# Decoder block with retrieved experts: four last rows fetched in halves, the last query-weight chunk moved into an up weight's place

## The chip, the cores and the metric

The kernel runs on one core of a Trainium2 chip. The metric is the device time of one execution in microseconds (us). TensorE (PE) multiplies matrices, VectorE (DVE) and ScalarE (ACT) work on tiles, GpSimd (POOL) issues the indirect gathers, SyncE (SP) issues the plain transfers, and 16 DMA engines move the bytes between HBM and SBUF.

## What is computed

One layer of a decoder block on 256 tokens of width 1024, in float32. The parts that matter here come late in it:

```python
mixed = jax.nn.sigmoid(g_a) * (y_a @ w_up_fox[l]) + jax.nn.sigmoid(g_b) * (y_b @ w_up_moba[l])
x = x + gate1 * (mixed @ w_out[l])
h2 = rms_norm(x, norm2_g[l]) * (1.0 + scale2) + shift2
x = x + gate2 * peer_ffn(h2, ...)
# peer_ffn, for each token:
q = h2 @ w_q                                  # 8 heads x 2 halves x 128
sc = einsum(q, sub_keys); s1, i1 = top_k(sc[0], 16); s2, i2 = top_k(sc[1], 16)
eid = the 16 best of the pairs (i1, i2)       # one expert of 16384 each
g = softmax of their scores
y = sum over 8 heads x 16 experts of g * gelu(h2 . u_tab[eid]) * v_tab[eid]
```

Each token thus reads 128 experts, each a U vector and a V vector of 1024 floats.

## The kernel before

The 256 tokens are two tiles (t = 0, 1) of 128, one token per partition. The first stages (modulation, input projection, attention) use matrix weights that SP streams through `ring`, four places of 2 MB. The last four such chunks are the two up weights (places 2 and 3 of `ring`) and the two output weights (places 0 and 1).

**Rows.** The experts are handled as `ROWS` = 256 rows: row n is, for every token of tile n // 128, its expert number n % 128. A gather brings U and V of one row for 128 tokens, 1 MB (8 KB per partition), into one *place*. For each row DVE takes the dot product of U with h2 (`dots`, L1010), ACT makes gelu, the weight and a diagonal matrix of it (L1285, L1290, L1297), and PE adds diagonal times V into `ps_y` (`add_rows`, L1611). ACT takes rows two at a time, and one at a time in the last four pairs (`ALONE`).

**Places.** `BUFFERS` lists the places with the row from which each takes part. `plan_buffers` deals them round: a place goes to the back of the line when it has been used, and a new one enters at the front at its row. A gather into a place used before waits until PE has added the row that it held (`s_added`); a first use waits for what occupied the memory (`await_first_use`). POOL issues all gathers in the order of rows, from one loop (L581). Places R0a to R3b are halves of the four places of `ring`; Ka and Kb are the memory `kz` of the keys of attention.

**Query weights.** `w_peer_q` comes in four chunks of 2 MB, loaded by SP (`peer_run`, L494). Chunk 0 lies in `K_chunk`, which is `kz`; chunk 3 comes into `kz` too, once the queries (t=1, m=1) have read chunk 0. Queries m = 2c and 2c+1 read chunk c. `SLOT` says before which pair of rows PE computes which queries: (0, 6) stands at pair 25, (1, 0) and (1, 1) at pairs 7 and 10, (1, 7) at pair 40.

**First rows.** After the queries (0, 0) `choose_first` (DVE) ranks the scores of head 0, and the first 8 experts follow from them. ACT had copied the scores from PSUM to `sc` before. Between there and the first row PE finishes tile 1: the up products `("up", 1, c, g)`, the turning of the mixed rows by `turn_wide(1, h)` (four transposes each, L1370, copied to SBUF by ACT at L1239) and `out_part(1, n)`, the items `("o", 1, 0)` and `("o", 1, 1)` (L1562). Place R2 is free after ("up", 1, 1, 0), R3 and G after ("up", 1, 1, 1), R0 after ("o", 1, 0), R1 after ("o", 1, 1), W and X when h2 of tile 1 is done.

**End.** The last `SPLIT` rows are gathered in halves: first U of each, then, behind all U, V of each. PE waits for V of such a row by `s_late_v`.

Of the kernel before, what the change touches and what calls it, by code (L numbers as in the profile page):

```python
# [14 lines left out]
P = 128  # L15
# [52 lines left out]
EARLY = 8  # L68
ROWS = 2 * HEADS * TOPK

SPLIT = 2

ALONE = 4

# [12 lines left out]
NORM2_ROOT = 1  # L87


BUFFERS = [("R2a", 0), ("R2b", 0), ("R3a", 0), ("R3b", 0), ("G", 0), ("R0a", 0), ("R0b", 0), ("R1a", 0),  # L90
           ("R1b", 0), ("W", 11), ("X", 12), ("V", 52), ("S", 53), ("E", 76), ("Ka", 88), ("Kb", 89)]


def plan_buffers():
# [79 lines left out]
def block_kernel(nc, x, small, b_ada, b_fgate, norm2_g, ada_t, in_t, up_t, out_t, peer_t, keys_t, peer_uv, out):  # L174
# [21 lines left out]
    with ExitStack() as ctx:  # L196
# [3 lines left out]
        def sem(name):  # L200
            return ctx.enter_context(nc.semaphore(name))

        ring = sb("ring", [P, NW, KD, 512])
# [14 lines left out]
        sc = sb("sc", [P, LISTS * P])  # L218
# [108 lines left out]
        def blocks_of(place):  # L327
# [3 lines left out]
                     [blocks_of(extra[:]), blocks_of(yT[:, 0].rearrange("p g b n -> p (g b n)")),  # L331
                      blocks_of(fx[:].rearrange("p a n -> p (a n)")),
                      blocks_of(score[:, 2].rearrange("p j n -> p (j n)"))],
                     [K_chunk]]
        peer_from = [[sum(run.shape[1] for run in runs[:r]) for r in range(len(runs) + 1)] for runs in peer_runs]

        def peer_block(m, k):
# [55 lines left out]
        s_sq4 = sem("x1_squares_summed")  # L393
        s_h2 = sem("h2_half_ready")
        s_warm = sem("root_of_one_ready")
        s_g0 = sem("top_scores_shifted")
        s_g1 = sem("top_scores_exp")
        s_eid = sem("expert_ids_ready")
# [21 lines left out]
        def await_item(eng, key):  # L420

            if key in turned_no:
                eng.wait_ge(s_turned, turned_no[key] + 1)
            else:
                eng.wait_ge(s_item, plan[key] + 1)
# [5 lines left out]
        def await_read(eng, key):  # L431

            if key in turned_no:
                eng.wait_ge(s_turned_read, turned_no[key] + 1)
            else:
                eng.wait_ge(s_bank[plan[key] % NB], plan[key] // NB + 1)
# [23 lines left out]
        def await_first_use(eng, name):  # L460

            if name in "VS":
                await_item(eng, ("qp", 1, 3))
            elif name == "E":
                await_item(eng, ("qp", 1, 5))
            elif name[0] == "K":
                await_item(eng, ("qp", 1, 7))
            elif name == "G":
                await_read(eng, ("up", 1, 1, 1))
            elif name in "WX":  # L470
                eng.wait_ge(s_h2, 2 * TILES)
            else:
                await_item(eng, {"0": ("o", 1, 0), "1": ("o", 1, 1), "2": ("up", 1, 1, 0), "3": ("up", 1, 1, 1)}[name[1]])

        def gates_done(u):

# [5 lines left out]
        @block.sync  # L482
        def _(sp):
            def chunk(n):
                what, m = chunks[n]
                if n >= NW:
                    await_chunk_read(sp, n - NW)
                dst = ring[:, n % NW, :, :]
                src = {"ada": ada_t, "z": in_t, "up": up_t, "out": out_t}[what][m]
                sp.dma_start(dst, src).then_inc(s_chunk[n % NW], 16)  # L490

            def peer_run(m, r):
                first, last = peer_from[m][r:r + 2]
                sp.dma_start(peer_runs[m][r], peer_t[m, :, first:last, :]).then_inc(s_peer[m], 16)  # L494

            sp.dma_start(sm[:], small).then_inc(s_small, 16)
            sp.dma_start(x_sb[:], x[0].rearrange("(t p) d -> p t d", p=P)).then_inc(s_x, 16)
            for n in range(ADA_FIRST - 1):
                chunk(n)
            n, part = ADA_FIRST - 1, KD // 2  # L500
            sp.dma_start(ring[:, n, 0:part, :], ada_t[n, :, 0:part, :]).then_inc(s_ada_half, 16)
            sp.dma_start(ring[:, n, part:KD, :], ada_t[n, :, part:KD, :]).then_inc(s_chunk[n], 16)
            sp.wait_ge(s_zero, 2)
            for r, at in zip(MOD_ROW, (2, 3, 4, 5)):
                sp.dma_start(rows[0:1, r, :], b_ada[0:1, at * D:(at + 1) * D]).then_inc(s_bias, 16)
            for n in range(ADA_FIRST, len(chunks)):
                chunk(n)
            await_block(sp, NZ * KD - 1)
            sp.dma_start(g2_row, norm2_g[0].partition_broadcast(P)).then_inc(s_g2, 16)
            sp.dma_start(skT[:], keys_t).then_inc(s_keys, 16)  # L510
            await_item(sp, ("S", 1, 1, HEAD_PAIRS - 1))
            sp.dma_start(x_sb[:], x[0].rearrange("(t p) d -> p t d", p=P)).then_inc(s_x, 16)
            peer_run(0, 0)
            await_item(sp, ("y", 1, 1, HEAD_PAIRS - 1))
            for r in range(2):
                peer_run(1, r)
            await_item(sp, ("up", 0, 1, 1))
            for r in range(1, 4):
                peer_run(2, r)
            sp.wait_ge(s_norm2_row, 1)  # L520
            peer_run(2, 0)
            await_item(sp, ("qp", 1, 1))
            peer_run(3, 0)
            for t in range(TILES):
                for h in range(2):
                    cut = slice(h * HALF, (h + 1) * HALF)
                    sp.wait_ge(s_yrow, 2 * t + h + 1)
                    sp.dma_start(out[0, t * P:(t + 1) * P, cut], x_sb[:, t, cut]).then_inc(s_stored, 16)
            sp.wait_ge(s_stored, 32 * TILES)
# [61 lines left out]
        def _(dve):  # L591
# [297 lines left out]

            def choose_first():  # L890

                await_read(dve, ("sc", 0, 0))
                for l in range(2):
                    ins = dve.max(v16[:, l, 0:EARLY], sc[:, l * P:(l + 1) * P])
                link(ins)
                for l in range(2):
                    ins = dve.max_index(i16[:, l, 0:EARLY], v16[:, l, 0:EARLY], sc[:, l * P:(l + 1) * P])
                link(ins)
                link(dve.tensor_copy(i16f[:, 0:2, 0:EARLY], i16[:, 0:2, 0:EARLY]))
                sums8 = flat[:, 0:EARLY * EARLY]  # L900
                link(dve.tensor_tensor(sums8.rearrange("p (a b) -> p a b", b=EARLY),
# [154 lines left out]
        def _(act):  # L1056
# [200 lines left out]
            def queries(t, m):  # L1257
                key = ("qp", t, m)
                await_item(act, key)
                read(act.activation(qp[:, m % 2, :, :],  # L1260
                                    bank(key)[:, 0:2 * P].rearrange("p (a n) -> p a n", n=P), ACT.Copy), key)
                if scored(t, m):
                    key = ("sc", t, m)
                    first, width = scored(t, m)[0], 2 * P * len(scored(t, m))
                    await_item(act, key)
                    if t:
                        act.wait_ge(s_eid, m + 2)
                    read(act.activation(sc[:, first * 2 * P:first * 2 * P + width],
                                        bank(key)[:, first % 2 * 2 * P:first % 2 * 2 * P + width], ACT.Copy), key)

# [78 lines left out]
        def _(pe):  # L1349
# [282 lines left out]
            up(1, 1, 0, first=1)  # L1632
            for c_ in range(2):
                up(1, c_, 1)
            for h in range(2):
                turn_wide(1, h)
            for n in range(2):
                out_part(1, n)
            for pair in range(NG * PAIRS):
                for stage in behind.get(pair, ()):  # L1640
                    stage()
# [53 lines left out]
```

## Time and profile before

| | |
|---|---|
| median of 3 runs | 904.52 us (904.2 to 905.95) |
| profiled execution: its time | 903.49 us |
| profiled execution: span from first to last instruction | 901.7 us |
| mean granted TensorE clock | 0.984 of full |
| PE busy | 772.4 us (86%) |
| DVE busy | 613.4 us (68%) |
| gathered by POOL's queue | 268.45 MB in 258 issues |
| mean transfer rate over the span | 373 GB/s |

All times in the text are counted from the start of the span. The time of an execution is 1.8 us above its span. A busy PE counts matmuls whose ends are modelled; the idle time of an engine that is not the bottleneck costs nothing.

### The profile page before, as it was taken

Reading aid. Unit: us, or ns where it says so; the run is one execution under the profiler, and the core shown is the slowest. Engines: PE = TensorE matmul, PEld = TensorE weight load, DVE = VectorE, ACT = ScalarE, POOL = GpSimd, SP = SyncE. Lnnn points to the kernel's source line nnn. Section 1 sums busy time; section 2 is a strip of 40 time slices with the busy share of each in tenths; the row PEclk is TensorE's granted clock in tenths of the full one; section 3 lists DMA queues with packets and bytes.
Section 4 is the critical chain, followed back from the end, with each engine's and each line's share of the span. In section 5 each row is a group of like instructions: output and inputs, shape, how many; then the busy total and the mean of one; then the engine's idle time right before and its main releaser. Section 6 shows DMA issues by size and latency. Waiting matters only on the chain.

```text
span 901.7 us, 8442 instructions
## 1 busy us (share of the span) xinstructions
PE 772.4 (86%) x2526; PEld 416.1 (46%) x2526; DVE 613.4 (68%) x1420; ACT 346.9 (38%) x1027; POOL 287.8 (32%) x279
## 2 busy tenths in 40 slices
PE   4999999999999999999997778687777777777777
PEld 2477777667556556565652333233322233222232
DVE  6788798954587967748669788768744444444445
ACT  3457688862144342422423242322422222222222
POOL 4000000000244444554636444353343334333320
PEclk9999999999999999999999989999999999999999
DMA  9977545679399999999999999999999999999995
GB/s 373 421 281 280 186 188 200 264 301 379 120 372 422 411 423 421 422 419 422 421 420 423 420 423 420 422 423 419 423 420 423 420 423 420 421 422 422 422 421 205
DMA packets 43812, 336.70 MB, mean 373 GB/s; under 512 B 4852, under 2 KB 4980, under 8 KB 7032
## 3 DMA queue, kind: packets, MB, share of 16 engines
q0 software_dynamic: 37152, 268.45, 71.9%
q1 hardware_dynamic: 6600, 67.72, 18.9%
q8 instruction: 20, 0.33, 0.1%
q14 instruction: 24, 0.20, 0.1%
q10 hardware_dynamic: 16, 0.00, 0.0%
HBM read 335.11 MB, written 1.05 MB: 373 GB/s over the span
## 4 chain that ended last, share of the span: by engine, by line
PE 47%; DMA 36%; DVE 10%; ACT 3%; issue 2%; POOL 1%; SPq 0%; DVEq 0%; ACTq 0%
DMA ring<-in_peer_uv,eid 26%; PE ps_y L1611 21%; DMA rows<-in_peer_uv,eid 6%; PE bank L1581 5%; DMA extra<-in_peer_uv,eid 4%; PE bank L1547 3%; DVE ring L1010 3%; PE bank L1422 2%; PE bank L1424 2%; PE bank L1423 2%; PE bank L1562 2%; PE ps_y L1422 1%; PE ps_y L1386 1%; PE ps_y L1424 1%; PE ps_y L1423 1%
## 5 line engine op out<-in xcount | busy, mean ns | idle before, releaser
L1611 PE MATMUL ps_y<-ring,diag 128*128 128x512 f32 x572 | 273.2, 617 | 58.2 <-ACT diag L1297 58.2
L581 POOL DMA_INDIRECT ring<-in_peer_uv,eid x142 | 150.1, 1057 | 414.8 <-DVE eid L916 227.0
L1010 DVE CUSTOM_DVE_ANT_0 ring<-ring,gates 128x1024 f32<-128x1024 f32 x143 | 173.2, 1224 | 101.8 <-DMA ring<-in_peer_uv,eid 101.0
L1611 PEld LDWEIGHTS ps_y<-ring,diag 128*128 128x128 f32 x572 | 108.0, 194 | 204.5 <-issue 116.8
L1285 ACT ACTIVATE mask<-mask 128x2 f32<-128x2 f32 (+1 forms) x132 | 26.7, 203 | 376.3 <-DVE mask L1010 376.1
L1297 ACT ACTIVATE diag<-ident,mask 128x128 f32<-128x128 f32 x256 | 87.3, 386 | 0.3
L1611 PE MATMUL ps_y<-rows,diag 128*128 128x512 f32 x136 | 63.8, 613 | 9.6 <-ACT diag L1297 9.6
L1290 ACT ACTIVATE mask<-g_sb,mask 128x1 f32<-128x1 f32 x256 | 61.9, 287 | 4.3
L1010 DVE CUSTOM_DVE_ANT_0 rows<-rows,gates 128x1024 f32<-128x1024 f32 x34 | 41.3, 1225 | 32.2 <-DMA rows<-in_peer_uv,eid 32.1
L645 DVE TENSOR_TENSOR w_lo<-ring,w_hi 128x512 fp32r<-128x512 f32 x76 | 50.6, 685 | 10.0 <-PE bank L1424 8.7
L1106 ACT ACTIVATE w_hi<-ring 128x512 fp32r<-128x512 f32 x76 | 45.6, 626 | 22.5 <-PE bank L1424 22.0
L581 POOL DMA_INDIRECT rows<-in_peer_uv,eid x34 | 37.8, 1111 | 31.2 <-PE ps_y L1611 26.7
L1611 PEld LDWEIGHTS ps_y<-rows,diag 128*128 128x128 f32 x136 | 25.6, 194 | 45.7 <-issue 27.3
L1611 PE MATMUL ps_y<-kz,diag 128*128 128x512 f32 x88 | 40.2, 599 | 7.5 <-ACT diag L1297 7.5
L1611 PE MATMUL ps_y<-gates,diag 128*128 128x512 f32 x72 | 34.8, 605 | 9.5 <-ACT diag L1297 9.5
L630 DVE SCALAR_TENSOR_TENSOR rows<-ring,silu,rows 128x512 f32<-128x512 f32 x56 | 41.9, 749 | 1.1
L1010 DVE CUSTOM_DVE_ANT_0 kz<-kz,gates 128x1024 f32<-128x1024 f32 x22 | 26.7, 1225 | 18.6 <-DMA kz<-in_peer_uv,eid 18.6
L1422 PE MATMUL bank<-w_hi,hT_hi 128*128 128x512 f32 x88 | 36.1, 410 | 0.0
L1424 PE MATMUL bank<-w_lo,hT_hi 128*128 128x512 f32 x88 | 34.3, 390 | 0.0
L1423 PE MATMUL bank<-w_hi,hT_lo 128*128 128x512 f32 x88 | 34.3, 390 | 0.0
L581 POOL DMA_INDIRECT kz<-in_peer_uv,eid x22 | 22.4, 1017 | 35.7 <-PE ps_y L1611 22.9
L1611 PE MATMUL ps_y<-spare,diag 128*128 128x512 f32 x52 | 25.2, 606 | 8.8 <-ACT diag L1297 7.6
(228 smaller groups left out, 1194.0 us busy)
## 6 DMA issues: line engine op xcount, KB each, us to landing
ring<-in_ada_t SPq DMA_DIRECT2D x11, 2048.0 KB, 9.6
ring<-in_in_t SPq DMA_DIRECT2D x10, 2048.0 KB, 10.1
ring<-in_up_t SPq DMA_DIRECT2D x2, 2048.0 KB, 8.7
ring<-in_out_t SPq DMA_DIRECT2D x2, 2048.0 KB, 13.7
kz<-in_peer_t SPq DMA_DIRECT2D x2, 2048.0 KB, 17.7
ring<-in_peer_uv,eid POOLq DMA_INDIRECT x142, 29.0
x_sb<-in_x SPq DMA_DIRECT2D x2, 1024.0 KB, 12.0
ring<-in_ada_t SPq DMA_DIRECT2D x2, 1024.0 KB, 21.3
```

Source lines behind the costliest of these rows:

```text
L581: pool.indirect_dma_start(uv_row(n), None, peer_uv, bass.IndirectOffsetOnAxis(ap=eid[:, n:n + 1], axis=0)).then_inc(s_uv[name], 16)
L630: ins = dve.scalar_tensor_tensor(out=acc, in0=w, scalar=silu[:, k:k + 1], in1=acc, op0=ALU.mult, op1=ALU.add)
L645: dve.tensor_tensor(w_lo[:, j % NLO, :], w, w_hi[:, j % NHI, :].bitcast(F32), ALU.subtract).then_inc(s_w_lo, 1)
L1010: dve.tensor_tensor_reduce(u_row(n), u_row(n), h2[:, n // P, :], 1.0, 0.0, ALU.mult, ALU.add, adot[:, at:at + 1]).then_inc(s_dot, 1)
L1106: act.activation(w_hi[:, j % NHI, :], ring[:, no % NW, k, :], ACT.Copy).then_inc(s_w_hi, 1)
L1290: act.activation(ew[:, c_:c_ + 1], g_sb[:, n:n + 1], ACT.Copy, scale=gel[:, c_:c_ + 1]).then_inc(s_ew, 1)
L1297: act.activation(diag[:, n % ND, :], ident[:], ACT.Copy, scale=ew[:, c_:c_ + 1]).then_inc(s_diag, 1)
L1422: pe.matmul(spot, hT_hi[:, k, at], hi, start=(k == 0), stop=False)
L1423: pe.matmul(spot, hT_lo[:, k, at], hi, start=False, stop=False)
L1424: ins = pe.matmul(spot, hT_hi[:, k, at], lo, start=False, stop=(k == KD - 1))
L1581: ins = pe.matmul(b[:, j * P:(j + 1) * P], peer_block(m // 2, k)[:, at:at + P], tT[:, t, k, :], start=(k == 0), stop=(k == KD - 1))
L1611: ins = pe.matmul(ps_y[:, cut], diag[:, n % ND, :], v_row(n)[:, cut], start=first, stop=last)
```

## The change

`SPLIT` goes from 2 to 4, so rows 252 to 255 come in halves. Chunk 3 of the query weights goes to `ring[:, 3]`, the place of the second up weight, and is loaded after ("up", 1, 1, 1). R3a and R3b take part from row 88 on instead of row 0, Ka and Kb from row 30 instead of row 88, W and X from rows 9 and 10 instead of 11 and 12. `choose_first` reads the scores from PSUM; ACT copies them after it. On PE the products of ("o", 1, 0) are halved around the second turning.

```diff
-SPLIT = 2
+SPLIT = 4
...
-BUFFERS = [("R2a", 0), ("R2b", 0), ("R3a", 0), ("R3b", 0), ("G", 0), ("R0a", 0), ("R0b", 0), ("R1a", 0),
-           ("R1b", 0), ("W", 11), ("X", 12), ("V", 52), ("S", 53), ("E", 76), ("Ka", 88), ("Kb", 89)]
+BUFFERS = [("R2a", 0), ("R2b", 0), ("G", 0), ("R0a", 0), ("R0b", 0), ("R1a", 0), ("R1b", 0), ("W", 9), ("X", 10),
+           ("Ka", 30), ("Kb", 31), ("V", 52), ("S", 53), ("E", 76), ("R3a", 88), ("R3b", 89)]
...
-                     [K_chunk]]
+                     [ring[:, 3, :, :]]]
...
             elif name[0] == "K":
-                await_item(eng, ("qp", 1, 7))
+                await_item(eng, ("qp", 1, 1))
...
-                await_item(eng, {"0": ("o", 1, 0), "1": ("o", 1, 1), "2": ("up", 1, 1, 0), "3": ("up", 1, 1, 1)}[name[1]])
+                await_item(eng, {"0": ("o", 1, 0), "1": ("o", 1, 1), "2": ("up", 1, 1, 0), "3": ("qp", 1, 7)}[name[1]])
...
-            await_item(sp, ("qp", 1, 1))
+            await_item(sp, ("up", 1, 1, 1))
             peer_run(3, 0)
...
             def choose_first():

-                await_read(dve, ("sc", 0, 0))
+                key = ("sc", 0, 0)
+                await_item(dve, key)
                 for l in range(2):
-                    ins = dve.max(v16[:, l, 0:EARLY], sc[:, l * P:(l + 1) * P])
+                    ins = dve.max(v16[:, l, 0:EARLY], bank(key)[:, l * P:(l + 1) * P])
                 link(ins)
                 for l in range(2):
-                    ins = dve.max_index(i16[:, l, 0:EARLY], v16[:, l, 0:EARLY], sc[:, l * P:(l + 1) * P])
-                link(ins)
+                    ins = dve.max_index(i16[:, l, 0:EARLY], v16[:, l, 0:EARLY], bank(key)[:, l * P:(l + 1) * P])
+                ins.then_inc(s_first, 1)
+                dve.wait_ge(s_first, 1)
...
                     if t:
                         act.wait_ge(s_eid, m + 2)
+                    elif m == 0:
+                        act.wait_ge(s_first, 1)
...
-            for h in range(2):
-                turn_wide(1, h)
-            for n in range(2):
-                out_part(1, n)
+            turn_wide(1, 0)
+            out_part(1, 0, (0,))
+            turn_wide(1, 1)
+            out_part(1, 0, (1,))
+            out_part(1, 1)
```

## Rows read from the trace of the kernel before

**Rows 1.** The page: GB/s by slice, the chain by engine, gathers issued (KB, us to landing)

```profile
GB/s 373 421 281 280 186 188 200 264 301 379 120 372 422 411 423 421 422 419 422 421 420 423 420 423 420 422 423 419 423 420 423 420 423 420 421 422 422 422 421 205
...
PE 47%; DMA 36%; DVE 10%; ACT 3%; issue 2%; POOL 1%; SPq 0%; DVEq 0%; ACTq 0%
...
ring<-in_peer_uv,eid POOLq DMA_INDIRECT x142, 29.0
```

**Rows 2.** Windows: length, PE, PEld, DVE, ACT, POOL busy, clock, DMA share, GB/s

```profile
258.00:262.00 4.00, 4.00 (x13) 1.86 (x12) 3.65 (x9) 2.53 (x8) 2.73 (x3) 1.00 0.83 281
...
266.00:316.00 50.00, 47.77 (x216) 29.61 (x217) 42.71 (x141) 19.87 (x58) 24.20 (x20) 1.00 1.01 417
...
332.00:887.00 555.00, 454.96 (x1229) 206.85 (x1227) 353.61 (x838) 165.27 (x595) 234.33 (x221) 0.98 1.01 421
```

**Rows 3.** Timeline of POOL: start us, us, engine, line, instruction, [idle before <-releaser]

```profile
242.70 0.93 POOL L581 DMA_INDIRECT ring<-in_peer_uv,eid  x1 [2.12 <-PE bank L1547]
...
251.79 0.94 POOL L581 DMA_INDIRECT ring<-in_peer_uv,eid  x1 [5.67 <-PE bank L1562]
253.03 1.51 POOL L581 DMA_INDIRECT ring<-in_peer_uv,eid  x1 [0.30 <-issue]
258.66 1.50 POOL L581 DMA_INDIRECT ring<-in_peer_uv,eid  x1 [4.11 <-PE bank L1562]
...
265.74 1.80 POOL L581 DMA_INDIRECT rows<-in_peer_uv,eid  x1 [1.75 <-DVE gates L870]
```

**Rows 4.** Timeline of SP: the issue of chunk 3

```profile
316.66 0.33 SPq L494 DMA_DIRECT2D kz<-in_peer_t  x1
```

**Rows 5.** Landing time of L581, issues starting at 238.2, 251.8, 258.7, 304.0

```profile
DMA to landing us min/median/max: 5.8/5.8/5.8
...
DMA to landing us min/median/max: 7.9/7.9/7.9
...
DMA to landing us min/median/max: 6.3/6.3/6.3
...
DMA to landing us min/median/max: 6.8/6.8/6.8
```

**Rows 6.** Timeline of PE: turnings and output products of both tiles

```profile
206.55 0.60 PE L1370 MATMUL bank<-ident,rows 128*128 128x128 f32 x4
207.93 3.69 PE L1562 MATMUL bank<-ring,tT 128*128 128x256 f32 x16 [0.78 <-ACT tT L1239]
...
242.27 0.60 PE L1370 MATMUL bank<-ident,rows 128*128 128x128 f32 x4
243.99 0.66 PE L1370 MATMUL bank<-ident,rows 128*128 128x128 f32 x4 [1.12 <-DVE rows L845]
244.49 13.90 PE L1562 MATMUL bank<-ring,tT 128*128 128x512 f32 x32
```

**Rows 7.** Timeline of ACT and DVE: first scores, and dots of rows 2, 3

```profile
233.02 0.38 ACT L1268 ACTIVATE sc<-bank 128x256 f32<-128x256 f32 x1 [0.86 <-PE bank L1591]
233.51 0.49 DVE L894 MAX8 v<-sc 128x8 f32<-128x128 f32 x2 [5.75 <-ACT sc L1268]
...
256.98 1.22 DVE L1010 CUSTOM_DVE_ANT_0 ring<-ring,gates 128x1024 f32<-128x1024 f32 x1
...
258.13 1.22 DVE L1010 CUSTOM_DVE_ANT_0 ring<-ring,gates 128x1024 f32<-128x1024 f32 x1
```

**Rows 8.** DVE's groups of instructions from 266 to 316: dots of rows in `ring`

```profile
L1010 DVE CUSTOM_DVE_ANT_0 ring<-ring,gates 128x1024 f32<-128x1024 f32 x14 | 16.6, 1220 | 0.1
```

**Rows 9.** Timeline of the end: dots of row 253, PE's rows 253 to 255

```profile
889.63 1.23 DVE L1010 CUSTOM_DVE_ANT_0 ring<-ring,gates 128x1024 f32<-128x1024 f32 x1 [1.23 <-DMA ring<-in_peer_uv,eid]
...
891.92 3.70 PE L1611 MATMUL ps_y<-ring,diag 128*128 128x512 f32 x8 [0.47 <-ACT diag L1297]
...
895.45 1.88 PE L1611 MATMUL ps_y<-v_sb,diag 128*128 128x512 f32 x4
```

**Rows 10.** Window of the last bytes, columns as in rows 2

```profile
893.00:894.00 1.00, 1.00 (x4) 0.45 (x3) 0.33 (x2) 0.65 (x4) 0.00 (x0) 1.00 0.07 29
```

More of the change, by code:

```diff
@@ L395, in block_kernel @@
         s_warm = sem("root_of_one_ready")
+        s_first = sem("first_scores_ranked")
         s_g0 = sem("top_scores_shifted")
```

## The prediction

> **What bounds the kernel now.** I read the page's rate line first. Between the eleventh slice (about 230 us) and the last the queues move 420 GB/s almost without a break [rows 1]: from the first gather on, this kernel is the transfer of 256 MB of rows. The windows say how full that is: 417 GB/s from 266 to 316 and 421 from 332 to 887, with the DMA share at 1.0, but 281 GB/s and a share of 0.83 from 258 to 262 [rows 2]. So a row (1.049 MB) costs 1.049 / 421 = 2.49 us, a half row 1.245, a chunk of 2.1 MB 4.98. The chain of waits names PE for 47% and DMA for 36% [rows 1]; where PE is named between 283 and 442 us the transfers are full beside it, so PE sets nothing there. The end can move by only three things: bytes after the gathers begin; time in which the DMA engines have nothing to do; what follows the last landing.
>
> The idle time lies before 262 us, and POOL's timeline says why. Rows 0 to 4 have free places. The gather into R0a then waits 5.67 us for PE's L1562 and the one into R1a another 4.11 us [rows 3]; these are the items ("o", 1, 0) and ("o", 1, 1). R1a is the last gather that finds the engines empty: it lands 6.3 us after its issue, against 5.8 for the very first gather, which met no other work [rows 5]. From its landing (258.66 + 6.3 = 264.9) until the end I count the DMA full. What the change does to the issue of R1a moves the end one for one.
>
> **The chunk and the places.** Before, R3a and R3b take 2 MB from 242.70 on [rows 3], and chunk 3 takes its 2 MB when (1, 1) is done: SP issues it at 316.66 [rows 4]. After, chunk 3 is issued at the moment at which R3a's gather was, and R3a and R3b drop out: the two change places. Ahead of R1a there are seven row-sized transfers in both kernels (before rows 0 to 6; after rows 0 to 4 and the chunk), and behind it the same 249: before 248 rows and the chunk, after 250 rows, less R1a itself. The 4.98 us that leave the full stretch come back as two rows that were not moved early. Sum: 0.
>
> The places after row 6 agree as well. Before, row n+2 waits for the adding of row n-9 (11 places); after, row n does (9 places). From row 30 both have 11, since Ka and Kb come in just as the chunk would have been issued. (1, 1) is at pair 10, so POOL, which for row 29 waits for the adding of row 20, has passed it already: no new wait at rows 30 and 31. R3a at row 88 waits for (1, 7), just as Ka did at row 88: 0. Queries 6 and 7 read the chunk from another place, at one price, and at pair 25 it has long landed.
>
> **First scores from PSUM.** DVE starts at 233.51 where ACT's copy began at 233.02 [rows 7]: rows 0 and 1 are issued 0.4 to 0.5 us sooner. Nothing comes of it, because the engines run empty again before R1a. The copy itself now lies behind the ranking, and DVE needs it only 10 us later. Should a PSUM operand cost DVE a few tenths, the same cover takes it. Worth 0, either way.
>
> **The halved product.** Before, PE turns half 0 at 242.27, waits 1.12 us for DVE, turns half 1 at 243.99 and runs 32 pieces without a hole from 244.49, 13.90 us, 0.434 each [rows 6]. ACT's copies hide: that of half 1 is ready before its product is due. After, the first 8 pieces start when copy 0 is in. From the first transpose to the first product that takes 207.93 - 206.55 = 1.38 us, as tile 0 shows [rows 6]: 242.27 + 1.38 = 243.65. They end at 247.12; turning 1 follows, and now its copy has nothing over it, because the next work is the half that needs it: 247.12 + 1.38 = 248.50. Tile 0 avoids this by putting parts 2 and 3 behind the turning. The other 24 pieces take 10.42: 258.92, against 244.49 + 13.90 = 258.39. So ("o", 1, 1) is 0.5 us later, and ("o", 1, 0), eight pieces behind 248.50, too (251.97 against 251.44).
>
> What hangs on it: POOL issues R0a at 252.3 instead of 251.79, and R1a at 259.2 instead of 258.66. The issue at 251.79 took 0.94 us; the next at 253.03, 1.51; those at 258.66 and 265.74, 1.50 and 1.80 [rows 3], and these three overlapped dots on DVE. R0a's issue now meets the dots of rows 0 and 1, which ran from 252.5 to 254.8; I give it 1.5 to 2.0 us. It landed 7.9 us after its issue while the engines were still busy with G [rows 5]; with chunk and G done by about 255 and R0a's descriptors at 254, I put the landing at 258.5 to 259. It is row 3 now, and row 3's dots stood at 258.13 [rows 7]: DVE is held 0.4 to 0.9 us. R1a's issue then runs between 1.0 and 1.5 us as before. Its shift is bounded below by about 0.1 (if it escapes the 0.5 us of DVE overlap that it has now) and above by 0.9 (all that DVE loses passes to it). I take 0.5, PE's own shift, as the nearest row.
>
> Here a rule weighs against the change. The row shows a stretching of 0.6 to 0.9 us beside dots [rows 3], and the issue at 253.03 ended at 254.54, before the dots did. The Trainium skill (SBUF — State Buffer, section "SBUF: two separate sides") says that a DVE instruction in a two-port mode shuts GpSimd out until it is done, so descriptors can't be written. By that R0a would be ready only at 254.8 + 0.94; the sum below takes the rows instead, and the full lock is a rival. The trace agrees in kind, not in size.
>
> **Two rows fewer in hand.** In this stretch row n lands when row n+2 landed before, 5 us later in PE's order. That would hurt if the dots followed the landings closely. They don't: from 266 to 316 the 14 dots in `ring` found their row there, with 0.1 us of idle time ahead of them all [rows 8]. The tightest gather before starts at 304.0 and lands 6.8 us later [rows 5], 1.0 us more than one that meets idle engines. If DVE and PE come 0.9 late and the DMA 0.5, that slack is 0.6: no hole. Cost 0, and one for one from a lateness of 1.5 us on.
>
> **The four halved rows.** Before: row 253 lands whole at 889.6, its dots start at 889.63, PE starts its row at 891.92 and row 255 at 895.45 [rows 9]: 1.72 us per row and 0.09 once. The last bytes move before 894 [rows 10]; 889.6 + 4 halves of 1.245 = 894.6 as their landing. So the end hangs on three rows of PE behind the dots of 253; V of 255 is there 0.9 us early. After: all four U land first (885.9, 887.1, 888.4, 889.6), and their dots and diagonals are ready by 892. V of 252 lands at 894.6 - 3 x 1.245 = 890.9. PE has nothing to do from 889 until then, and four rows to do after: 890.9 + 0.1 + 3 x 1.72 + 0.09 = 896.2 for the start of row 255, against 895.45. That is 0.75 us later. Halves carry bytes at the whole rows' rate or they would not have landed in time before; two more issues cost POOL 1.2 us each at a point where a gather waits some 29 us to land, median of the 142 into `ring` [rows 1]. Bounds: 0.4 if V of 252 comes a little earlier than its share, 1.0.
>
> **Sum.** Chunk 0, places 0, scores 0, halved product +0.5 (0.1 to 0.9), tail +0.75 (0.4 to 1.0): +1.25, from 0.5 to 1.9. The profiled execution took 903.49, so 904.7 on its scale; the median is 1.0 above it, so 904.52 + 1.25 = 905.8.
>
> **Rivals.** A measurement here tells about 0.2%, 1.8 us.
> - *The start does not shift* (R1a escapes the overlap, or PE closes the hole): only the tail, 905.3. Chance 0.20, no change.
> - *Faster: the chunk travels for nothing.* From the landing of row 0 (244.0) to that of R1a (264.9) are 20.9 us for seven rows, 17.4 us of work: 3.5 us are idle. If chunk 3 filled them and the rows were not late for it, -3.5 + 0.75 = -2.75, 901.8. It decides only if R1a or its followers are issued earlier than now. Against it: POOL's waits at 251.79 and 258.66 are on PE. Chance 0.08.
> - *Slower: nine places starve the transfers* between rows 9 and 29. From 1.5 us of lateness on, each further one is idle DMA. At 3.5 us: 0.5 + 2.0 + 0.75 = 3.25, 907.8. For it: DVE's chain from 265 to 283 has no hole in which to recover. Against: the slack above. Chance 0.13.
> - *Full lock of GpSimd* (the skill's page named above): R0a's descriptors at 255.75, landing with 5.8 - 0.94 behind at 260.6, the dots of row 3 late by 2.5; then 1.0 us of starving: 0.5 + 1.0 + 0.75 = 2.25, 906.8. Chance 0.07.
>
> **Numbers.** Forecast as summed 0.52, of which 0.08 at its upper edge passes 1.8 us. Faster 0.08; same 0.44 + 0.20 = 0.64; slower 0.13 + 0.07 + 0.08 = 0.28. Range 903.8 to 907.8, from part of the way to the faster case up to the starved one; the forecast's own range is 905.0 to 906.5.
>
> **What the profile after would show.** A hole of some 0.7 us on PE between the second turning and L1562 near 248 us; POOL's R1a issue near 259.2, with a duration above 1 us for R0a; the chunk landing near 252 to 255 and none at 330; full windows from 266 on, above all no dip between 290 and 316; at the end PE waiting for the DMA at row 252 and then four rows in 7 us. A window under 400 GB/s between 270 and 330, or R1a issued before 258, would prove the forecast wrong, and so would a last PE row that starts as close to the last landing as before (0.9 us).

## The result and the profile after

The changed kernel took 907.72 us (median of 8 runs, 905.9 to 908.49) against 904.86 us for the kernel before (8 runs, 904.11 to 905.95): ratio 1.003, interval 1.0021 to 1.0039. That is 2.7 us more, from 1.9 to 3.5, and slower by more than the 0.2% that a measurement tells. The forecast was 905.8; the time lies 0.08 us inside the upper edge of the range, beside the rival "nine places starve". A time slower by more than 1.8 us had been given a chance of 0.28. The profiled execution after is the lowest of its eight: 905.9 us, a span of 903.8, against 903.49 and 901.7 before. The rows below thus explain 2.1 of its 2.4 us; the second profile further down has a span longer by 4.8.

The other 0.3 us lie outside the span. Of the kernel before, all executions take 1.8 to 1.9 us more than their span. Of the kernels with four halved rows, all 48 take 2.1 to 2.2 more, and of those with two or three, 84 executions, 1.8 to 1.9. So four halved rows cost 0.3 us that no row of a profile shows; what it is stays open.

The page after: the rate by slice, the chain by engine, the gathers into `ring`, as in [rows 1].

```profile
GB/s 376 418 279 279 187 186 199 265 306 370 149 326 422 417 410 422 420 421 421 421 421 421 420 423 421 420 422 421 422 422 421 421 421 422 421 422 421 422 420 202
...
PE 43%; DMA 40%; DVE 7%; ACT 3%; POOL 3%; issue 3%; another core or an unknown queue 1%; POOLq 0%; SPq 0%; DVEq 0%; ACTq 0%
...
ring<-in_peer_uv,eid POOLq DMA_INDIRECT x132, 27.1
```

The picture is the same, but the eleventh and twelfth slice together carry 475 GB/s instead of 492, and the fifteenth 410 instead of 423. The next fence is PE after: the turnings and output products (L1375 and L1567 are L1370 and L1562 of before), to be held against [rows 6].

```profile
242.47 0.60 PE L1375 MATMUL bank<-ident,rows 128*128 128x128 f32 x4
243.84 3.67 PE L1567 MATMUL bank<-ring,tT 128*128 128x512 f32 x8 [0.78 <-ACT tT L1242]
247.35 0.60 PE L1375 MATMUL bank<-ident,rows 128*128 128x128 f32 x4
248.73 10.54 PE L1567 MATMUL bank<-ring,tT 128*128 128x512 f32 x24 [0.78 <-ACT tT L1242]
```

The hole in front of the second stretch is 0.78 us, and that stretch starts 0.03 us from where I had put it once the 0.20 by which this execution starts later is taken off (248.50 + 0.20). POOL's gathers, then the dots of rows 2 and 3 on DVE, after:

```profile
252.68 1.89 POOL L582 DMA_INDIRECT ring<-in_peer_uv,eid  x1 [7.73 <-PE bank L1567]
254.87 0.94 POOL L582 DMA_INDIRECT ring<-in_peer_uv,eid  x1 [0.30 <-issue]
259.54 1.72 POOL L582 DMA_INDIRECT ring<-in_peer_uv,eid  x1 [3.74 <-PE bank L1567]
...
320.94 0.93 POOL L582 DMA_INDIRECT gates<-in_peer_uv,eid  x1 [5.35 <-PE ps_y L1616]
322.17 1.98 POOL L582 DMA_INDIRECT kz<-in_peer_uv,eid  x1 [0.30 <-issue]
```

```profile
256.99 1.23 DVE L1013 CUSTOM_DVE_ANT_0 gates<-gates 128x1024 f32<-128x1024 f32 x1
259.23 1.23 DVE L1013 CUSTOM_DVE_ANT_0 ring<-ring,gates 128x1024 f32<-128x1024 f32 x1 [1.00 <-DMA ring<-in_peer_uv,eid]
```

The reader sees three things. R0a's issue, now beside the dots of rows 0 and 1, took 1.89 us; DVE then waited 1.00 us for that gather, which is row 3 now; and the gather of row 29 waited 5.35 us for PE's adding, with Ka's right behind it at 322.17. The transfers, columns as in [rows 2]:

```profile
290.00:316.00 26.00, 25.50 (x112) 15.40 (x111) 21.93 (x77) 9.00 (x30) 11.28 (x10) 1.00 1.01 417
316.00:332.00 16.00, 15.97 (x75) 10.04 (x75) 11.98 (x23) 6.07 (x18) 8.93 (x8) 1.00 1.00 403
332.00:887.00 555.00, 455.23 (x1235) 207.58 (x1234) 354.49 (x837) 164.51 (x592) 232.05 (x224) 0.98 1.01 421
```

and the two short windows of the kernel before:

```profile
290.00:316.00 26.00, 25.50 (x112) 15.40 (x111) 22.93 (x80) 8.99 (x30) 11.27 (x10) 1.00 1.01 412
316.00:332.00 16.00, 15.97 (x72) 9.80 (x71) 11.82 (x21) 6.34 (x19) 7.24 (x6) 1.00 1.01 424
```

From 332 on both move 421 GB/s [rows 2]. Between 316 and 332 the changed kernel moves 21 GB/s less, which is 16 x 21 / 421 = 0.8 us of transfer. The end, to be held against [rows 9]: dots of row 251, then PE's rows 252 and 255.

```profile
885.91 1.22 DVE L1013 CUSTOM_DVE_ANT_0 rows<-rows,gates 128x1024 f32<-128x1024 f32 x1 [1.26 <-DMA rows<-in_peer_uv,eid]
...
892.31 1.95 PE L1616 MATMUL ps_y<-extra,diag 128*128 128x512 f32 x4 [2.14 <-DMA extra<-in_peer_uv,late_id]
...
897.54 1.88 PE L1616 MATMUL ps_y<-v_sb,diag 128*128 128x512 f32 x4
```

PE waits 2.14 us for V of row 252 and then has four rows to add, as forecast.

**One measure for all profiles.** In 14 profiles PE's first turning of tile 1 started anywhere from 242.2 to 244.05 us, whatever the kernel, and ahead of it none of the changes shows on its path. So I cut each span into the time of that turning, a *middle* from there to the dots of row 251 (the last row that all kernels gather whole), and a *tail* from there to PE's start on row 255. Before: 242.27 + 642.37 + 10.81 = 895.45. After: 242.47 + 643.44 + 11.63 = 897.54; the parts differ by 0.20, 1.07 and 0.82. "Row 3" is the start of its dots after the turning.

| kernel | median | ratio to before (interval) | turning | row 3 | middle | tail |
|---|---|---|---|---|---|---|
| before | 904.86 | | 242.27 | 15.86 | 642.37 | 10.81 |
| after | 907.72 | 1.003 (1.0021 to 1.0039) | 242.47 | 16.76 | 643.44 | 11.63 |
| after, again | 908.36 | 1.0039 (1.0024 to 1.0053) | 243.53 | 16.74 | 645.09 | 11.67 |
| after, two halved rows | 906.24 | 1.0016 (1.0007 to 1.0025) | 243.50 | 16.59 | 644.27 | 10.80 |
| after, old product order | 907.41 | 1.0035 (1.0023 to 1.0047) | 242.82 | 17.38 | 644.99 | 13.33 |
| chunk and scores alone | 906.17 | 1.0015 (1.0006 to 1.0024) | 242.31 | 17.57 | 645.90 | 10.85 |
| four halved rows alone | 906.01 | 1.0019 (1.001 to 1.0028) | 242.51 | 15.86 | 642.95 | 11.61 |
| halved product alone | 904.68 | 1.0004 (0.9994 to 1.0013) | 243.83 | 15.86 | 642.62 | 10.78 |
| chunk in place 1 | 905.49 | 1.0007 (0.9998 to 1.0016) | 244.05 | 15.87 | 643.82 | 10.78 |
| before, DVE made late | 906.73 | 1.0025 (1.0014 to 1.0037) | 243.01 | 17.71 | 644.37 | 10.76 |
| after, K a row earlier | 906.99 | 1.0019 (1.001 to 1.0028) | 243.65 | 16.57 | 644.41 | 11.58 |
| chunk in place 1, K a row earlier | 904.44 | 0.9993 (0.9984 to 1.0002) | 242.20 | 15.86 | 643.49 | 10.76 |
| before, chunk handed over late | 905.2 | 0.9996 (0.9987 to 1.0005) | 243.65 | 15.86 | 642.84 | 10.77 |
| before, mixed order of halves | 904.93 | 0.9998 (0.9989 to 1.0007) | 243.24 | 15.86 | 643.00 | 10.64 |

Ratios were taken between runs on the same chip. One profile is one execution: the five with rows and chunk as before and DVE left alone have middles of 642.37 to 643.00, mean 642.76, so a middle is good to some 0.3 us, and against the 642.37 of the kernel before, the lowest of the five, a difference comes out up to 0.4 us too large.

### The profile page after: what moved, and what is told of

Its sections match the earlier page's. It is cut to its first block, busy times and chain, and to the rows that moved or that the text cites. A ratio compares the mean times of both kernels' runs of the same rounds, so it can differ in the third digit from the quotient of the medians.

```text
span 903.8 us, 8450 instructions
## 1 busy us (share of the span) xinstructions
PE 772.5 (85%) x2526; PEld 416.1 (46%) x2526; DVE 613.8 (68%) x1420; ACT 346.7 (38%) x1027; POOL 284.7 (31%) x281
## 4 chain that ended last, share of the span: by engine, by line
PE 43%; DMA 40%; DVE 7%; ACT 3%; POOL 3%; issue 3%; another core or an unknown queue 1%; POOLq 0%; SPq 0%; DVEq 0%; ACTq 0%
DMA v_sb<-in_peer_uv,eid 22%; PE ps_y L1616 15%; DMA rows<-in_peer_uv,eid 14%; PE bank L1586 5%; DMA extra<-in_peer_uv,late_id 3%; PE bank L1552 3%; PE bank L1567 2%; PE bank L1427 2%; PE bank L1429 2%; PE bank L1428 2%; PE ps_y L1427 1%; PE ps_y L1391 1%; PE ps_y L1429 1%; PE ps_y L1428 1%; POOL ring L582 1%
## 5 line engine op out<-in xcount | busy, mean ns | idle before, releaser
L1616 PE MATMUL ps_y<-ring,diag 128*128 128x512 f32 x528 | 246.2, 612 | 49.5 <-ACT diag L1302 49.5
L582 POOL DMA_INDIRECT ring<-in_peer_uv,eid x132 | 137.5, 1042 | 404.3 <-DVE eid L919 226.8
L1013 DVE CUSTOM_DVE_ANT_0 ring<-ring,gates 128x1024 f32<-128x1024 f32 x132 | 159.7, 1225 | 103.5 <-DMA ring<-in_peer_uv,eid 103.0
L1616 PEld LDWEIGHTS ps_y<-ring,diag 128*128 128x128 f32 x528 | 99.2, 194 | 187.9 <-issue 106.1
L1616 PE MATMUL ps_y<-kz,diag 128*128 128x512 f32 x120 | 56.0, 598 | 8.1 <-ACT diag L1302 8.1
L1013 DVE CUSTOM_DVE_ANT_0 kz<-kz,gates 128x1024 f32<-128x1024 f32 x30 | 36.7, 1223 | 24.8 <-DMA kz<-in_peer_uv,eid 24.7
L582 POOL DMA_INDIRECT kz<-in_peer_uv,eid x30 | 33.9, 1130 | 25.3 <-PE ps_y L1616 21.2
L1616 PEld LDWEIGHTS ps_y<-kz,diag 128*128 128x128 f32 x120 | 22.1, 190 | 38.8 <-issue 24.6
L1616 PEld LDWEIGHTS ps_y<-gates,diag 128*128 128x128 f32 x76 | 15.2, 214 | 47.5 <-ACT diag L1302 33.1
L582 POOL DMA_INDIRECT gates<-in_peer_uv,eid x18 | 18.3, 1018 | 51.1 <-PE ps_y L1616 46.9
```

The costliest lines, as they stand in the source:

```text
L582: pool.indirect_dma_start(uv_row(n), None, peer_uv, bass.IndirectOffsetOnAxis(ap=eid[:, n:n + 1], axis=0)).then_inc(s_uv[name], 16)
L1013: dve.tensor_tensor_reduce(u_row(n), u_row(n), h2[:, n // P, :], 1.0, 0.0, ALU.mult, ALU.add, adot[:, at:at + 1]).then_inc(s_dot, 1)
L1616: ins = pe.matmul(ps_y[:, cut], diag[:, n % ND, :], v_row(n)[:, cut], start=first, stop=last)
```

## The experiments

**The changed kernel again, and with two halved rows.** The first has no edit.

> The changed kernel unaltered, for a second profile. Its first one showed the end 2.1 us later in the span: PE's last row starts at 897.54 against 895.45. Theory A (start and tail): 0.75 us of that is the tail of four halved rows, the rest (1.2 to 1.4) came in before 332 us by the late gather into R1a. The median of its runs was 2.9 us over the kernel before, so a profile of a run nearer the median should show where the other 0.7 to 1.5 us come from. A: R1a's issue or the tail is still later than in the first profile. Rival B (nine places starve the transfers): windows between 266 and 332 us below 415 GB/s.

```diff
-SPLIT = 4
+SPLIT = 2
```

> The changed kernel with two halved rows instead of four; all else as changed. A: the last row of PE starts 0.9 us behind the last landing instead of 1.7, total 0.75 us less than the changed kernel (0.5 to 1.0). Rival C (the end is set by the landings alone): no difference.

The second profile of the changed kernel is 2.7 us slower than the first. Its windows show a stretch in which TensorE was granted 0.83 of full speed on the mean, a mixture of its two levels 2.4 and 1.2 GHz (0.50 of full from 286 to 288 us). PE had just waited 2.06 us for a diagonal, and the clock fell within 0.6 us of its first piece behind that pause. Behind the stretch the transfers starve:

```profile
285.40 3.68 PE L1616 MATMUL ps_y<-ring,diag 128*128 128x512 f32 x4 [2.06 <-ACT diag L1302]
...
280.00:290.00 10.00, 7.94 (x15) 3.17 (x14) 8.72 (x18) 4.81 (x14) 3.08 (x3) 0.83 1.02 424
290.00:316.00 26.00, 25.50 (x112) 15.44 (x111) 19.25 (x76) 7.60 (x29) 11.42 (x11) 1.00 0.96 376
```

26 x (421 - 376) / 421 = 2.8 us of transfer are missing there. With two halved rows the tail is 10.80 us, as before, and the time falls to 906.24, by 1.5 and 2.1 us against the two medians of the change, more than the 0.5 to 1.0 expected: 0.8 of it is the tail and 0.3 lies outside the span. About half of the loss remained.

**Chunk and scores alone; the old product order alone.** The first undoes the halved product and the four halved rows, the second only the product. Both have this edit to the changed kernel, the first SPLIT = 2 as well:

```diff
-            turn_wide(1, 0)
-            out_part(1, 0, (0,))
-            turn_wide(1, 1)
-            out_part(1, 0, (1,))
-            out_part(1, 1)
+            for h in range(2):
+                turn_wide(1, h)
+            for n in range(2):
+                out_part(1, n)
```

> The changed kernel with both undone, two halved rows and the product in one piece: what is left of the change is the chunk's move with its places and the scores read from PSUM. A: equal to the kernel before within 0.3 us, transfers full from 266 us on. B: 1 us or more slower than before, with windows below 415 GB/s between 270 and 332 us. Rival D (the chunk travels for nothing): 2 to 3 us faster than before.

> The changed kernel with the product (o, 1, 0) in one piece behind both turnings, as before the change. A: the gather into R0a is issued before the dots of rows 0 and 1 and takes 0.94 us again, the dots of row 3 wait for nothing or for 0.3 us, R1a is issued at 258.7 to 258.9 instead of 259.5; total 0.9 to 1.3 us less than the changed kernel. B: less than 0.3 us saved, since the nine places cost it.

What I had priced at 0 costs 1.4 us (0.5 to 2.2) by itself. Row 3 is late without the halved product too. The profile of chunk and scores alone: dots of row 3, the pause of PE near 283 us, then the windows, with a half-clock stretch like the one above.

```profile
259.88 1.23 DVE L1013 CUSTOM_DVE_ANT_0 ring<-ring,gates 128x1024 f32<-128x1024 f32 x1 [1.79 <-DMA ring<-in_peer_uv,eid]
...
284.88 2.45 PE L1616 MATMUL ps_y<-ring,diag 128*128 128x512 f32 x4 [2.66 <-ACT diag L1302]
...
280.00:290.00 10.00, 7.34 (x14) 2.87 (x13) 8.23 (x17) 4.36 (x14) 3.45 (x3) 0.83 1.01 421
290.00:316.00 26.00, 25.51 (x113) 15.53 (x112) 19.68 (x74) 8.13 (x29) 11.05 (x10) 1.00 0.92 345
```

Here the last window is 4.7 us of transfer short of 421 GB/s. The old product order in the changed kernel gained nothing that can be told (907.41): R1a goes out 16.38 us after the turning instead of 17.07. R0a, too, is issued earlier (252.34 in this trace, 9.52 after the turning, against 10.21), but lands 7.8 us later instead of 6.5, so that row 3 comes at 17.38 instead of 16.76, after a wait of 1.61 us where none or 0.3 was expected; no run shows why it lands later. Time is lost behind it:

```profile
290.00:316.00 26.00, 25.51 (x113) 15.40 (x112) 21.02 (x76) 9.01 (x30) 10.89 (x11) 1.00 0.98 377
```

Its tail of 13.33 us holds a stretch of PE at the lower level, 0.50 granted from 896 to 898 us, behind 2 us of waiting for V of row 252; it tells nothing of the order.

**Four halved rows alone; the halved product alone**, each put into the kernel before.

> The kernel before with four halved rows and nothing else. A (tail is PE's four rows behind V of row 252): last landing unchanged, PE idle for about 2 us ahead of row 252, its last row 1.6 to 1.7 us behind the last landing instead of 0.9: 0.75 us slower. What speaks for more: undoing the four rows in the changed kernel gave back 1.3 to 2 us in the median.

```profile
885.46 1.22 DVE L1010 CUSTOM_DVE_ANT_0 ring<-ring,gates 128x1024 f32<-128x1024 f32 x1 [1.26 <-DMA ring<-in_peer_uv,eid]
...
891.85 1.96 PE L1611 MATMUL ps_y<-extra,diag 128*128 128x512 f32 x4 [2.12 <-DMA extra<-in_peer_uv,late_id]
...
897.07 1.88 PE L1611 MATMUL ps_y<-v_sb,diag 128*128 128x512 f32 x4
```

The tail is 0.80 us longer and its rows repeat those of the change. The timing says 1.7 (0.9 to 2.5). The tail and the 0.3 us outside the span make 1.1, well within that; the middle, 0.58 above that of before and 0.2 above the mean of the five, is within the spread, so whether the halves cost more stays open.

> The kernel before with the product (o, 1, 0) halved around the second turning. A: both output items 0.5 us later, R0a's issue stretched to 1.9 us beside the dots of rows 0 and 1, but R0a is row 5 here and its dots come at 265: DVE isn't held. R1a 0.5 to 0.9 us later: total 0.5 to 0.9 us slower. Rival E (the halved product does not matter, since giving it back in the changed kernel saved nothing): 0 within 0.3 us.

The time rose by 0.4 us (-0.5 to 1.2), the middle by 0.25: a price of nothing isn't excluded. R1a's issue comes 17.07 us after the turning against 16.39 before, but takes 0.94 instead of 1.50 us, so that it ends only 0.1 later. It starts just as the dots of row 3 are over. POOL:

```profile
254.04 0.93 POOL L581 DMA_INDIRECT ring<-in_peer_uv,eid  x1 [6.35 <-PE bank L1562]
255.27 1.97 POOL L581 DMA_INDIRECT ring<-in_peer_uv,eid  x1 [0.30 <-issue]
260.90 0.94 POOL L581 DMA_INDIRECT ring<-in_peer_uv,eid  x1 [3.66 <-PE bank L1562]
```

Row 3 is on time (15.86), because in this kernel it lies in R3b and not behind the chunk.

**The chunk at R1's place in the order.** To take away row 3's lateness and keep the nine places, the chunk goes to place 1 of `ring`, behind ("o", 1, 1), and R3 holds rows from the start (beside SPLIT = 2 and the old product order):

```diff
-BUFFERS = [("R2a", 0), ("R2b", 0), ("G", 0), ("R0a", 0), ("R0b", 0), ("R1a", 0), ("R1b", 0), ("W", 9), ("X", 10),
-           ("Ka", 30), ("Kb", 31), ("V", 52), ("S", 53), ("E", 76), ("R3a", 88), ("R3b", 89)]
+BUFFERS = [("R2a", 0), ("R2b", 0), ("R3a", 0), ("R3b", 0), ("G", 0), ("R0a", 0), ("R0b", 0), ("W", 9), ("X", 10),
+           ("Ka", 30), ("Kb", 31), ("V", 52), ("S", 53), ("E", 76), ("R1a", 88), ("R1b", 89)]
...
-                     [ring[:, 3, :, :]]]
+                     [ring[:, 1, :, :]]]
...
-                await_item(eng, {"0": ("o", 1, 0), "1": ("o", 1, 1), "2": ("up", 1, 1, 0), "3": ("qp", 1, 7)}[name[1]])
+                await_item(eng, {"0": ("o", 1, 0), "1": ("qp", 1, 7), "2": ("up", 1, 1, 0), "3": ("up", 1, 1, 1)}[name[1]])
...
-            await_item(sp, ("up", 1, 1, 1))
+            await_item(sp, ("o", 1, 1))
```

> The chunk's move with its nine places, but into the place of the second output weight (R1) behind (o, 1, 1); R3a and R3b take part from row 0 again and R1a, R1b from row 88. Two halved rows, product in one piece, scores from PSUM. Rows 0 to 6 land as in the kernel before. Theory F (the chunk ahead of G and R0a makes row 3 land after its turn; DVE is held, h2 and all of PE are late, and only then do nine places starve the transfers): dots of row 3 at 258.0 without a wait, windows from 290 to 316 us back at 412 GB/s or more, total equal to the kernel before within 0.4 us, or up to 1 us faster as the chunk needs no descriptors of POOL. B (nine places starve by themselves): windows from 290 to 316 us near 350 to 380 GB/s as with the chunk in R3, 1 us or more slower than before.

Row 3 is on time, and the cost is 0.6 us (-0.2 to 1.4) instead of 1.4 (0.5 to 2.2). The intervals overlap, and the plain medians (905.49 against 904.3) differ by 1.2, so the fall points the right way and isn't proven. The windows are still short:

```profile
290.00:316.00 26.00, 25.51 (x113) 15.40 (x112) 21.34 (x76) 8.99 (x30) 11.08 (x10) 1.00 1.00 402
316.00:332.00 16.00, 15.97 (x75) 10.04 (x74) 11.62 (x23) 6.07 (x18) 8.82 (x8) 1.00 0.98 391
```

**DVE made late in the kernel before.** Four chained idle operations ahead of the dots of rows 2 and 3; they leave their data as it is.

```diff
+                if pair == 1:
+                    for _ in range(4):
+                        link(dve.tensor_tensor(dist[:], dist[:], dist[:], ALU.max))
```

> The kernel before with four idle operations of DVE (128x256, 0.42 us each, in a chain) ahead of the dots of rows 2 and 3: about 1.8 us of lateness and no other change; places and chunk as before. F: DVE and PE run 1.8 us late from there, the gathers that are issued near 294 and 304 us come too late, windows from 295 to 315 us fall below 400 GB/s, total 0.8 to 1.5 us slower. A (end set by R1a's landing and the tail): 0 to 0.5 us.

```profile
257.73 1.81 DVE L1050 TENSOR_TENSOR dist<-dist 128x256 f32<-128x256 f32 x4
259.57 1.23 DVE L1010 CUSTOM_DVE_ANT_0 ring<-ring,gates 128x1024 f32<-128x1024 f32 x1
...
270.00:290.00 20.00, 16.75 (x73) 9.85 (x72) 18.35 (x59) 9.09 (x26) 10.39 (x9) 1.00 0.98 386
...
280.00:290.00 10.00, 7.35 (x23) 3.41 (x22) 9.07 (x20) 5.29 (x14) 6.52 (x4) 1.00 0.96 356
...
290.00:316.00 26.00, 25.50 (x112) 15.39 (x111) 20.44 (x75) 8.89 (x30) 11.30 (x11) 1.00 1.00 402
```

With nothing of the change in it and with eleven places, 1.85 us of lateness at row 3 cost 2.3 us (1.3 to 3.3) by time and 2.0 by the middle (1.6 against the mean of the five). This is the run that settles the disputed step: DVE has no slack of 1.5 us there. With a slack of 1.5 and one for one behind it, 0.35 us would have been lost. As an estimate from the lower end of the interval, the slack is at most 1.85 - 1.3 = 0.6 us if the rest is lost one for one; what the 0.9 us of the change itself costs, no run measures. The transfers ran short from 280 to 290 us, 356 GB/s against 420 before, earlier than I had expected.

**Ka and Kb one row earlier**, in the changed kernel and in the one with the chunk in place 1:

```diff
-            ("Ka", 30), ("Kb", 31), ("V", 52), ...
+            ("Ka", 29), ("Kb", 30), ("V", 52), ...
```

> The changed kernel with Ka and Kb one row earlier (29 and 30 instead of 30 and 31). Theory G: in the changed kernel POOL reaches Ka only behind row 29, whose place comes free with the adding of row 20, 5.3 us (79.7 against 74.4 us after the first turning) after the moment at which the kernel before handed chunk 3 to the queues; the transfers run short of work there (395 GB/s from 320 to 330 us). With row 29 in Ka, POOL issues it at 74.6: windows from 320 to 330 us at 420 GB/s, dots of row 34 0.4 to 0.9 us earlier after the turning than in the changed kernel, total 0.3 to 0.9 us less. Rival A (places 0): nothing changes.

> The chunk in R1's place (the dots of row 3 find their row), two halved rows, product in one piece, and Ka and Kb from rows 29 and 30. G with F: both losses of the move are gone, total equal to the kernel before within 0.4 us or up to 0.7 us faster; the landing of row 251 after the first turning at 642.4 to 643.0 us, where the chunk in R1 alone had 643.8. B (nine places starve by themselves): as the chunk in R1 alone, 0.6 us over the kernel before.

Ka's gather no longer stands behind one that waits for an adding: after the turning, the gathers of rows 28, 29 and 30 start at 71.76, 75.33 and 77.13 us, against 71.99, 78.47 and 79.70 in the changed kernel. The window from 316 to 332 is full again, here with the chunk in place 1:

```profile
290.00:316.00 26.00, 25.51 (x112) 15.41 (x112) 23.00 (x80) 8.99 (x30) 11.27 (x10) 1.00 0.98 379
316.00:332.00 16.00, 15.97 (x71) 9.80 (x71) 10.98 (x20) 6.43 (x20) 10.13 (x8) 1.00 1.01 423
```

The changed kernel so edited took 906.99 us, the other 904.44: about 1 us less than its partner each time, with intervals that overlap. The second is the best version found, and not to be told from the kernel before (-0.6 us, -1.4 to 0.2), although its middle, 643.49, lies above the 642.4 to 643.0 expected. Its window from 290 to 316, at 379 GB/s, is 2.6 us of transfer short of 421. A low window alone is thus no loss of that size: from 230 to 290 us this kernel had moved 330 GB/s against 322 before, 0.5 MB or 1.1 us of transfer ahead.

**The chunk handed over late, in the kernel before.**

```diff
             await_item(sp, ("qp", 1, 1))
+            sp.wait_ge(s_added, 21)
             peer_run(3, 0)
```

> The kernel before, but SP hands chunk 3 to the queues only when row 20 has been added, 3 to 5 us later than before. G: the queues run short between 320 and 330 us as in the changed kernel, 0.4 to 1 us slower. A: 0.

```profile
320.99 0.33 SPq L494 DMA_DIRECT2D kz<-in_peer_t  x1
```

Issued 3.0 us later after the turning than before (77.34 against 74.39), the chunk cost nothing (-0.4 us, -1.2 to 0.5). A transfer late by 3.0 us at this point is covered as long as eleven places stand around it; a lateness of 5.3 us, as that of Ka, was not tried there.

**A mixed order of halves, in the kernel before.** Three halved rows, and V of 253 goes ahead of U of 255.

```diff
-SPLIT = 2
+SPLIT = 3
...
+                    if late:
+                        late_v(late - 1)
...
-            for late in range(SPLIT):
-                pool.indirect_dma_start(
-                    v_row(ROWS - SPLIT + late), None, halves,
-                    bass.IndirectOffsetOnAxis(ap=late_id[:, 1, late:late + 1], axis=0)).then_inc(s_late_v[late], 16)
+            late_v(SPLIT - 1)
```

> The kernel before with three halved rows and another order of the halves: U253, U254, V253, U255, V254, V255. By the sum that gave the tail of four rows (measured 0.8 us, PE 1.72 us a row, a half 1.245 us): PE adds row 253 3.6 us ahead of the last landing, 254 behind its V at -1.15, 255 at +0.6 us behind the last landing instead of +0.9: 0.3 us faster, too little to be timed; the profile should show 10.5 us from the landing of row 251 to the start of row 255 instead of 10.8. If the order does not matter: 10.8 or, as with three halved rows in the old order, 11.0.

```profile
895.09 1.96 PE L1616 MATMUL ps_y<-ring,diag 128*128 128x512 f32 x4 [0.37 <-DMA ring<-in_peer_uv,late_id]
896.88 1.88 PE L1616 MATMUL ps_y<-v_sb,diag 128*128 128x512 f32 x4
```

The tail is 10.64 instead of 10.81 us: the right direction, too little to time.

## Why the prediction was right, and where it was not

**Tail.** Right in mechanism and size within the span: +0.77 to +0.86 us in four profiles, against 0.75 forecast. PE's wait, the four rows behind it and the landing of V came as worked out. The forecast had nothing for the 0.3 us that four halved rows add outside the span, so their price is 1.1 us, above the bound of 1.0.

**Halved product.** Right in mechanism: the hole, the stretched issue beside dots (1.89 us; I gave it 1.5 to 2.0), and dots of row 3 held by 0.90 us (0.4 to 0.9 forecast). Its price alone is 0.4 us by time (-0.5 to 1.2) and 0.25 by the middle, against 0.5; the runs tell it neither from 0.5 nor from nothing. The end of R1a's issue moved by 0.1 us in the kernel with the halved product alone and by 0.9 in the changed kernel, where the late dots of row 3 stand beside it: the two bounds that I had given. What I hadn't seen is that the chunk alone holds row 3, and by more: 1.71 us. My rows had it: R0a landed 7.9 us after 251.79 [rows 3, rows 5], at 259.7, and row 3's dots stood at 258.13 [rows 7]. With the old order in the changed kernel R1a is earlier, but the loss behind row 3 stays.

**Full lock of GpSimd.** The 2.5 us of that rival did not come, but the lock did, for one instruction at a time:

```profile
252.53 1.22 DVE L1013 CUSTOM_DVE_ANT_0 ring<-ring,gates 128x1024 f32<-128x1024 f32 x1
```

R0a's issue started at 252.68, beside these dots of row 0, and ended at 254.57: 0.82 us behind their end at 253.75, although the dots of row 1 ran from 253.68 to 254.90. R1a's issue ended 0.81 us behind the end of row 3's dots before (260.16 and 259.35) and 0.80 after (261.26 and 260.46). Of the 815 gather issues of over 1.00 us in the 14 profiles, 801 end 0.81 us (0.805 to 0.821) behind the end of one DVE instruction that they met: dots in 696 cases, a TENSOR_TENSOR in 105. The other 14 are the first gather of each profile. The Trainium skill (SBUF — State Buffer, section "SBUF: two separate sides") has GpSimd shut out until a DVE instruction in a two-port mode is done. The trace agrees with it in the wait for one instruction; whether these dots run in such a mode, no run tells. What was wrong is my reading: "a stretching of 0.6 to 0.9 us" is the rest of one dot product that the issue sits out, and the rival made R0a wait for both dot products and then take its whole 0.94 us again.

**Scores from PSUM.** Right: 0.50 us for two rankings against 0.49 [rows 7], and nothing came of the earlier start. It was not run apart from the chunk.

**The step that failed: the places.** "No hole. Cost 0, and one for one from a lateness of 1.5 us on." The chunk's move, with the scores from PSUM, costs 1.4 us (0.5 to 2.2), in three ways that the runs bear out to different degrees:

1. *There was no slack of 1.5 us.* The chunk travels ahead of R0a, so R0a's gather, due at row 5 before, is due at row 3. It misses its turn by 0.7 to 1.7 us in all six profiles with the chunk in place 3, and 1.85 us of such lateness cost 2.3 in the kernel before. My evidence was that the dots from 266 to 316 found their rows there [rows 8]. That shows that DVE and PE run behind the transfers; then a later adding frees each place later, and the transfers starve (356 GB/s from 280 to 290 us with DVE made late). Here rows that were always in time were a sign that the engines set the pace, and the chain of waits had named PE there; I set it aside because the transfers were full beside it. Taking the lateness away left 0.6 us, with the overlap of intervals told above.
2. *Lateness widens a pause of PE, and behind it the clock can fall.* Near 283 us PE waits for a diagonal: 1.73 us before and at most 1.80 in eight others, but 1.98 and 2.06 in the two profiles of the change and 2.65 or 2.66 in three others whose row 3 is late by 1.5 to 1.9 us. In two of these five, with 2.06 and 2.66, TensorE fell to its lower level as PE went on, the next two rows took PE 5.2 us instead of 3.5, and the window behind was 2.8 and 4.7 us short. Two of five against none of nine is too few to show that the pause brings the fall. Both had nine places; the one kernel with eleven and a wide pause kept its clock, so that nine do worse there is argued and not shown.
3. *The wait at row 29 holds row 30.* I wrote that POOL has "passed it already". That took the rows before row 30 to be issued when the chunk was, but row 29's gather waits for the adding of row 20, 5.35 us, and POOL issues in order: Ka followed at 322.17, where SP, on a queue of its own, had issued the chunk at 316.66 [rows 4]. One row earlier repairs the window; a chunk late by 3.0 us in the kernel before costs nothing. Its own size, about 1 us by the two pairs of times with overlapping intervals, isn't settled, nor whether it would count with eleven places.

**The sum.** 1.4 for the chunk, 0.4 for the product, 0.8 for the tail and 0.3 outside the span make 2.9 us, against 2.7 (1.9 to 3.5) measured; with 1.7 for the four halved rows, as timed alone, it would be 3.5. Forecast were 0, 0.5 and 0.75. That the time lies within the range is in part luck: the upper edge came from the rival "nine places starve", which asked for 3.5 us of lateness, and its mechanism took part with 0.7 to 1.7 us. A slip in my count of the bytes did no harm: behind R1a there are 250 row-sized transfers in both kernels, not 249.

**What was to be seen.** Four of my signs came true: the hole, R0a's long issue, the chunk early (issued at 242.66, landed 11.1 us later), and the four rows at the end. The fifth, no window under 400 GB/s from 270 to 330, fails in the second profile of the change (376), and the first has 395 between 320 and 330.

## What to carry to other kernels

Before a buffer is lent to a transfer that now goes ahead of others, list for each later transfer which item it serves, and compare its landing with that item's turn: the count of bytes can be equal and the order still costs. Consumers that never wait for data are no slack where they free the buffers that the transfers wait for; an idle operation of known length in the unchanged kernel shows in one run whether lateness costs. A gather put behind a waiting one on an in-order queue inherits its wait, which the same transfer on another queue does not. And an execution can be longer than its span by an amount that the change alters: compare both.

## What the runs showed of the hardware

- TensorE was granted a lower clock near 286 us, on the mean 0.83 from 280 to 290, in 2 of 14 profiles, both times within 1.5 us of PE's going on after a pause (2.06 and 2.66 us); the next two rows took it 5.2 us instead of 3.5. Three profiles with pauses of 1.98 to 2.66 us there kept the full clock. The forecast had no term for this. One more profile fell to the lower level near 896 us, behind a pause of 2.1 us.
- Work ahead of the first turning, on whose path no change shows, varied by 1.8 us between executions (242.2 to 244.05 us), as much as most of the effects looked for. Only parts counted from a common event made the profiles comparable.
- A gather's issue that met a dot product on DVE took up to 2.0 us against 0.94 alone: it ended 0.81 us behind the end of that one dot product, whether or not the next one had begun.
- With four halved rows the time of an execution was 2.1 to 2.2 us above its span, with two or three 1.8 to 1.9.
